# A hybrid GLA and neighbourhood-attention step: gate tiles dealt over five steps, and probabilities divided by their sums ahead of the transposes

## The chip, the cores and the metric

The kernel runs on one core of one Trainium2 chip. The metric is the device time of one execution in microseconds (us), lower is better; the median of the runs is compared.

## What is computed

One layer of a diffusion backbone over 512 latent tokens (an 8 x 64 grid) and 128 context tokens, width 1024, all in fp32. The reference, cut to what the change touches:

```python
gq, gk, gv, gr, zf, zb, nq, nk, nv, m_gla, m_na = split_in(h @ w_in)
b_gla = (rmsnorm(o_gla, g_gla) * silu(gr)) @ w_gla_o            # 4 heads of 128
qn, kn = rmsnorm(nq, g_qn), rmsnorm(nk, g_kn)                   # 8 heads of 64
# neighbourhood attention: 8 x 16 window of the grid plus all 256 past context keys
s = concat([q k_rows * scale + bias, q k_ctx * scale])
p = softmax(s)
o = p_loc v_rows + p_ctx v_ctx
mix = (sigmoid(m_gla) * b_gla + sigmoid(m_na) * (o @ w_na_o)) @ w_out
```

Context tokens attend to the 128 context tokens alone.

## The kernel before, in words

The kernel is one program of five queues, written out by hand: PE (matmul), ACT, DVE, POOL and SP (its DMA queue), which wait for each other by semaphores. The activations lie transposed (channels in partitions, 640 tokens in the free dimension). A product in fp32 accuracy is made of three fast ones: each operand is split into a high and a low part (fp32r), and `project` (L638 to L653) issues hi x hi, hi x lo and lo x hi for each of 8 row blocks k of a weight tile: six matmuls of 320 columns for each k. A weight tile comes by SP's DMA into `wraw`, ACT's `hi` writes `whi`, and POOL's `lo` (L503) writes `wlo`.

The change lies in the attention stage. It has 20 steps s, four groups j of five: group j handles two heads (r = 0, 1), and i = s % 5 says which queries. For i = 0 to 3 they are 128 latent tokens (a group of 16 grid columns) that see 2, 3, 3 and 2 near blocks of 128 keys and 2 past blocks; for i = 4 they are the context tokens and see one block. In step s:

- PE issues `scores(s)` into the PSUM tensor PA (near blocks of head r in bank r, the past blocks of both heads in bank 2; L924, L928), then `probabilities(s-1)`, the transposes of the exponentials `sc` by a product with the identity (L946), then `gate_part(s)`, then `values(s-1)`, the products with v (L965).
- DVE takes the scores from PSUM, adds the bias, and finds the row maxima (L1991, L1993, L1999), head by head. Between the heads `sums(s-1)` forms the reciprocal of the previous step's sums and widens it to 64 columns for each head (L1964, L1967).
- PE transposes this widened tile too (L956), ACT copies it to `rin_t` (L1435), and DVE's `normalised` multiplies the values by it into `ona` (L1957).
- ACT copies the transposed exponentials to `pT` (L1406, L1408) and forms the exponentials with their sums (L1415).

`gate_part` is independent work for PE: the eight tiles of the projection for the gate m_gla, two in each group, each cut in two halves of 4 k, at i = 1 to 4. At i = 0 stands `gla_stats` instead, the statistics of one GLA head (L893, into PSUM tensor PJ, which the gate tiles also use); ACT's `gla_rms` (L1367, L1369), DVE's `gla_gate` at i = 1 (L1925, L1928), ACT's `gla_hi` at i = 2 and DVE's `gla_low` at i = 3 (L1920) process it. When a group's heads are complete, ACT's copy to `ona_hi` and DVE's `pair_low` (L1942) split them. POOL adds the masks to the bias table of the next group (three additions, L560) once the maxima of its i = 3 step are there, and then does the `lo` of the next two gate tiles. Before step 0 PE forms four statistics of q and k (L882), ACT their logarithms and exponentials (L1377, L1383), and DVE applies them in `qk_norm(n)` (L1933), n = 0 before the loop and n = 1 to 3 at steps 1 to 3, ahead of the maxima. After step 19 SP may load `ada_rest` (L440, waits for `pv_cp` 20), and the merge follows, whose first projection surrounds `values(19)`.

## Time and profile before

| | us |
|---|---|
| median of three runs | 1044.33 (1043.95 to 1046.63) |
| the profiled execution's own time | 1046.15 |
| its span | 1044.3 |
| PE busy | 1009.4 (97% of the span) |
| DVE, ACT, POOL busy | 566.8, 434.8, 478.7 |
| share of PE in the chain that ended last | 66% |

How to read it: the profile is one execution; times in a timeline are microseconds from the start of its span. A matmul's row lasts until its modelled end, and matmuls overlap, so a piece of PE's work is measured from the start of its first row to the start of the next piece's. Where an engine stood idle, the row says for how long and what released it.

### The profile page before, as it was taken

What the parts mean: (1) busy time and instruction counts of PE and PEld (TensorE: products, weight loads), DVE (VectorE), ACT (ScalarE), POOL (GpSimd) and SP (SyncE); (2) the same over time, 40 slices, a digit from 0 to 9 for tenths busy, and PEclk for the clock granted to TensorE, in tenths of its full rate; (3) what the DMA queues carried; (4) which work ended last, traced back from release to release, by engine and by line L of the source; (5) the groups of instructions that cost most, each with busy time, mean ns of one, the idle gap of its engine ahead of it and who ended that gap; (6) DMA issues with size and microseconds to landing.
All of it is one profiled execution on the core that took longest, in us unless ns stands there. A gap on an engine that the chain in (4) does not pass through costs nothing.

```text
span 1044.3 us, 18987 instructions
## 1 busy us (share of the span) xinstructions
PE 1009.4 (97%) x7435; PEld 935.3 (90%) x7435; DVE 566.8 (54%) x1069; ACT 434.8 (42%) x676; POOL 478.7 (46%) x305
## 2 busy tenths in 40 slices
PE   4999999999999999999999999899999999999998
PEld 3999999998788988999987899899999999788886
DVE  6408269842665653332324799777777778532102
ACT  4244254423756563222232355555555555521110
POOL 1476522223133211333342277788877786333331
PEclk9999999999999999999999999999999999999999
DMA  9964222121011006565525122232222231122231
GB/s 340 300 102 81 81 62 61 42 71 52 11 42 41 22 22 201 182 213 192 189 82 181 41 81 73 77 92 84 82 82 81 82 102 42 61 81 80 79 117 68
DMA packets 130837, 103.70 MB, mean 99 GB/s; under 512 B 5830, under 2 KB 111179, under 8 KB 130763
## 3 DMA queue, kind: packets, MB, share of 16 engines
q1 hardware_dynamic: 125736, 95.14, 29.5%
q0 software_dynamic: 1568, 3.15, 2.0%
q10 hardware_dynamic: 3459, 4.40, 1.2%
q8 instruction: 50, 0.82, 0.3%
q14 instruction: 24, 0.20, 0.1%
HBM read 98.21 MB, written 3.41 MB: 97 GB/s over the span
## 4 chain that ended last, share of the span: by engine, by line
PE 66%; POOL 17%; DVE 6%; issue 3%; DMA 3%; ACT 3%; SPq 2%; DVEq 0%; POOLq 0%; ACTq 0%
PE PJ L646 10%; PE PJ L647 10%; PE PJ L651 10%; POOL behind L606 7%; POOL ahead L606 4%; PE PA L1044 3%; PE PA L1045 3%; PE PA L1043 3%; PE PJ L1043 2%; PE PJ L1044 2%; PE PJ L1045 2%; POOL ahead_val L614 2%; PE PA L965 2%; PE PJ L946 2%; POOL behind_val L614 2%
## 5 line engine op out<-in xcount | busy, mean ns | idle before, releaser
L503 POOL TENSOR_TENSOR wlo<-wraw,whi 128x1024 fp32r<-128x1024 f32 x72 | 181.3, 2518 | 363.2 <-ACT whi L1221 268.4
L646 PE MATMUL PJ<-h_hi,whi 128*128 128x320 f32 x640 | 196.4, 315 | 0.0
L647 PE MATMUL PJ<-h_lo,whi 128*128 128x320 f32 x640 | 193.0, 309 | 0.0
L651 PE MATMUL PJ<-h_hi,wlo 128*128 128x320 f32 x640 | 145.9, 309 | 0.0
L646 PEld LDWEIGHTS PJ<-h_hi,whi 128*128 128x128 f32 x640 | 120.4, 188 | 2.6 <-issue 1.6
L647 PEld LDWEIGHTS PJ<-h_lo,whi 128*128 128x128 f32 x640 | 120.6, 188 | 0.0
L1221 ACT ACTIVATE whi<-wraw 128x1024 fp32r<-128x1024 f32 x51 | 53.9, 1059 | 147.7 <-PE PJ L651 78.4
L651 PEld LDWEIGHTS PJ<-h_hi,wlo 128*128 128x128 f32 x640 | 107.2, 188 | 0.0
L1597 ACT ACTIVATE whi<-wraw 128x1024 fp32r<-128x1024 f32 x21 | 22.2, 1059 | 105.6 <-PE PJ L1045 54.0
L2162 DVE SCALAR_TENSOR_TENSOR PJ<-u_all,vec,PJ 128x641 f32<-128x641 f32 x44 | 39.1, 888 | 41.8 <-ACT PJ L1549 41.8
L1164 PE MATMUL PA<-h_hi,behind 128*128 128x320 f32 x192 | 59.3, 309 | 0.0
L606 POOL TENSOR_TENSOR behind<-behind_val,behind 128x512 fp32r<-128x512 f32 x40 | 51.4, 1307 | 1.1 <-ACT behind L1576 1.1
L560 POOL TENSOR_TENSOR bias<-bias,window 128x512 f32<-128x512 f32 (+1 forms) x12 | 19.6, 1658 | 64.8 <-DVE mx_loc L1993 64.8
L1045 PE MATMUL PA<-whi,prod_lo 128*128 128x512 f32 x124 | 48.3, 389 | 0.0
L1162 PE MATMUL PA<-h_hi,ahead 128*128 128x320 f32 x128 | 40.7, 318 | 1.6 <-DVE u_all L2236 0.6
L1576 ACT ACTIVATE behind<-behind_val 128x512 fp32r<-128x512 f32 x40 | 25.0, 625 | 40.1 <-POOL behind_val L614 37.7
L1549 ACT ACTIVATE PJ<-u_all,vec 128x641 f32<-128x641 f32 x44 | 38.9, 884 | 4.6 <-DVE u_all L2228 2.5
L1162 PE MATMUL PA<-h_hi,behind 128*128 128x320 f32 x128 | 39.6, 310 | 0.5 <-issue 0.5
L2165 DVE SCALAR_TENSOR_TENSOR PJ<-u_all,vec,PJ 128x641 f32<-128x641 f32 x44 | 39.2, 890 | 1.5
L1163 PE MATMUL PA<-h_lo,ahead 128*128 128x320 f32 x128 | 39.6, 309 | 0.0
L1163 PE MATMUL PA<-h_lo,behind 128*128 128x320 f32 x128 | 39.6, 309 | 0.0
L1162 PE MATMUL PA<-T_hi,ahead 128*128 128x320 f32 x128 | 39.6, 309 | 0.0
(438 smaller groups left out, 2816.0 us busy)
## 6 DMA issues: line engine op xcount, KB each, us to landing
wraw<-in_w_in_dram SPq DMA_DIRECT2D x82, 256.0 KB, 3.1
ada_rest<-in_w_ada_dram SPq DMA_DIRECT2D x32, 512.0 KB, 5.8
wraw<-in_w_up_dram SPq DMA_DIRECT2D x48, 256.0 KB, 3.6
wraw<-in_w_down_dram SPq DMA_DIRECT2D x42, 256.0 KB, 2.9
raw_even<-in_w_up_dram SPq DMA_DIRECT2D x40, 256.0 KB, 3.6
ada<-in_w_ada_dram SPq DMA_DIRECT2D x8, 1024.0 KB, 9.6
wraw<-in_w_out_dram SPq DMA_DIRECT2D x16, 256.0 KB, 2.8
out_dram<-x ACTq DMA_DIRECT2D x10, 256.0 KB, 2.1
```

The costliest lines, as they stand in the source:

```text
L503: pool.tensor_tensor(wlo[:, slot, 0:k, :], wraw[:, slot, 0:k, :], whi[:, slot, 0:k, :].bitcast(F32), ALU.subtract).then_inc(lo_done, 1)
L606: pool.tensor_tensor(unit_lo[name], value_of(j, name), unit_hi[name].bitcast(F32), ALU.subtract).then_inc(lo_done, 1)
L646: pe.matmul(out, whi[:, slot, w0 + k, :], hi(k)[:, tok], start=start and k == k0, stop=False)
L647: pe.matmul(out, whi[:, slot, w0 + k, :], lo(k)[:, tok], start=False, stop=False)
L651: mm = pe.matmul(out, wlo[:, slot, w0 + k, :], hi(k)[:, tok], start=False, stop=stop and k == k1 - 1)
L1043: pe.matmul(psum(*bank), act_hi_[:, k, tok], w_hi, start=start, stop=False)
L1044: pe.matmul(psum(*bank), act_hi_[:, k, tok], w_lo, start=False, stop=False)
L1045: return pe.matmul(psum(*bank), act_lo_[:, k, tok], w_hi, start=False, stop=stop)
L1162: pe.matmul(out, w_hi[:, k, :], b_hi[:, k, :], start=k == 0, stop=False)
L1163: pe.matmul(out, w_hi[:, k, :], b_lo[:, k, :], start=False, stop=False)
L1164: mm = pe.matmul(out, w_lo[:, k, :], b_hi[:, k, :], start=False, stop=k == 3)
L1221: act.activation(whi[:, slot, :, :], wraw[:, slot, :, :], ACT.Copy).then_inc(hi_done, 1)
```

## The change

- The gate tiles are dealt over all five steps of a group (`GATE_K`): 2, 3 and 3 k for the first tile and 4 and 4 for the second.
- `weights(s)` on DVE multiplies the exponentials themselves (128 x 128 to 128 x 640 for each head) by the reciprocals of their sums, first thing in step s + 1, and PE's transposes wait for it. The widened tile, its transpose and `rin_t` are gone, and `values_out` on ACT copies the finished values.
- Where a step has two near blocks, the past blocks lie in the same bank as the near ones of their head, and the wait on `past_ps` is gone.
- `gla_stats` goes to PA; at i = 0 it follows the gate part, and the scores of i = 1 wait for its logarithm. The fourth q/k statistic moves behind the scores of step 0. On ACT its logarithm and `gla_rms(0)` come before the loop, two exponentials go into steps 1 and 2, and the copy to `ona_hi` comes one step earlier. On DVE `qk_norm(1..3)` and `pair_low` move behind the maxima.

```diff

-GATE_K = {1: (0, 0, 4), 2: (0, 4, 8), 3: (1, 0, 4), 4: (1, 4, 8)}
+GATE_K = [(0, 0, 2), (0, 2, 5), (0, 5, 8), (1, 0, 4), (1, 4, 8)]
 N_LEVEL = 8
...
         rin = at("rin", R + 143072, [2, 2])
-        rin_wide = at("rin_wide", R + 3584, [2, HD])
-        rin_t = at("rin_t", R + 4096, [P])

...
+        def past_at(i, r):
+
+            return 2 * BANK + r * PAST if KEYS[i][1] == 3 else r * BANK + 2 * P
         def halves(ps, pair):
...
-            for n in range(4):
+            def qk_stats(n):
+
                 pe.wait_ge(sqq_set, n + 1)
...
                 elif n >= 2:
-                    pe.wait_ge(sq_ln, n - 1)
+                    pe.wait_ge(sq_ln, 2 * n - 3)
                 for x in range(2):
...
                         o = (2 * x + b) * BANK
-                        mm = pe.matmul((PJ if n % 2 == 0 else PA)[:, o:o + HALF], blk64[:, :],
+                        mm = pe.matmul((PA if n == 1 else PJ)[:, o:o + HALF], blk64[:, :],
                                        qk_rs[n][:, x, b * HALF:(b + 1) * HALF], start=True, stop=True)
...
+            for n in range(3):
+                qk_stats(n)
+
             def gla_stats(hd):
...
                 pe.wait_ge(og_sqd, hd + 1)
-                pe.wait_ge(gate_cp, 2 * hd)
-                if hd == 0:
-                    pe.wait_ge(sq_ln, 4)
+                pe.wait_ge(sc_mx, 10 * hd + 2)
                 for b in range(2):
-                    mm = pe.matmul(PJ[:, b * BANK:b * BANK + HALF], ones[:, :], og_rs[:, b * HALF:(b + 1) * HALF],
+                    mm = pe.matmul(PA[:, b * BANK:b * BANK + HALF], ones[:, :], og_rs[:, b * HALF:(b + 1) * HALF],
                                    start=True, stop=True)
...
                 if s == 0:
-                    pe.wait_ge(sq_ln, 4)
+                    pe.wait_ge(sq_ln, 2)
                 else:
                     pe.wait_ge(sc_mx, 2 * s)
+                if i == 1:
+                    pe.wait_ge(og_ln, j + 1)
                 near = [(0, b) for b in range(nt)]
...
                     for r, (kind, b) in ((0, first), (1, second)):
-                        if r == 0 and kind == 1 and b == 0:
-                            pe.wait_ge(past_ps, j * 4 + i + 1)
+                        if r == 0 and kind == 1 and b == 0 and nt == 3:
+                            pe.wait_ge(past_ps, j * 2 + i)
                         hs = slice(64 * r, 64 * r + 64)
...
                         else:
-                            o = 2 * BANK + r * PAST + b * P
+                            o = past_at(i, r) + b * P
                             mm = pe.matmul(PA[:, o:o + P], q, kcT[hs, j, b * P:(b + 1) * P], start=True, stop=True)
-                            if r == 1 and b == 1:
+                            if r == 1 and b == 1 and nt == 3:
                                 mm.then_inc(past_ps, 1)
...
                 nb = KEYS[i][1] + 2 if i < 4 else 1
-                pe.wait_ge(sc_exp, 2 * s + 2)
+                pe.wait_ge(weight_set, s + 1)
                 if s:
...
                 pe.wait_ge(pt_cp, s + 1)
-                pe.wait_ge(wide_set, s + 1)
                 if s:
                     pe.wait_ge(pv_cp, s)
-                pe.transpose(PA[:, 3 * BANK + P:3 * BANK + 2 * P], rin_wide[:, :, :].rearrange("p r n -> p (r n)"), ident[:, :])
                 col = [(2 * j + r) * HD for r in range(2)]
...
                 j, i = s // 5, s % 5
-                if i == 0:
-                    gla_stats(j)
-                    return
                 b, k0, k1 = GATE_K[i]
                 n = 2 * j + b
+                if s == 0:
+                    qk_stats(3)
+                    gla_stats(0)
+                    pe.wait_ge(sq_ln, 4)
                 if k0 == 0:
-                    pe.wait_ge(og_ln, j + 1)
                     pe.wait_ge(gate_cp, n)
...
                         start=k0 == 0, stop=k1 == 8, done=tile_ready if k1 == 8 else None)
+                if i == 0 and s:
+                    gla_stats(j)
...
             qk_ln(2)
-            qk_ln(3)
             qk_exp(1)
             gla_square(0)
-            qk_exp(2)
-            qk_exp(3)
+            qk_ln(3)
+            gla_rms(0)
             act.wait_ge(nvt_cp, NT)
...
+            def values_out(s):
+
+                i = s % 5
+                act.wait_ge(pv_ps, s + 1)
+                if s == 0:
+                    act.wait_ge(stored, 32)
+                elif i == 0:
+                    act.wait_ge(on_lo, s // 5)
+                o = PA[:, 3 * BANK:3 * BANK + P]
+                if i < 4:
+                    act.activation(ona[:, 0:SAMPLE].rearrange("p (r g c) -> p g r c", g=4, c=GC)[:, i],
+                                   o.rearrange("p (r c) -> p r c", c=GC), ACT.Copy).then_inc(pv_cp, 1)
+                else:
+                    act.activation(ona[:, SAMPLE:TOK], o, ACT.Copy).then_inc(pv_cp, 1)
             on_constant()
-            for s in range(22):
+            for s in range(21):
                 i = s % 5
...
                                        accum_out=psm[:, s % 2, r:r + 1]).then_inc(sc_exp, 1)
-                    if i == 0:
+                    if i == 0 and s:
                         gla_rms(s // 5)
+                    if s in (1, 2):
+                        qk_exp(s + 1)
                     if i in (2, 4):
...
                 if 1 <= s <= 20:
-                    act.wait_ge(pv_ps, s)
-                    act.activation(rin_t[:, :], PA[:, 3 * BANK + P:3 * BANK + 2 * P], ACT.Copy).then_inc(rint_set, 1)
+                    values_out(s - 1)
                 if s < 20 and i == 2:
...
                     gla_square(s // 5 + 1)
-                if s >= 6 and i == 1:
-                    act.wait_ge(pv_cp, s - 1)
+                if s >= 5 and i == 0:
+                    act.wait_ge(pv_cp, s)
                     act.activation(ona_hi[:, s // 5 - 1, :], ona[:, :], ACT.Copy).then_inc(on_hi, 1)
...
-            def normalised(s):
-
-                i = s % 5
-                dve.wait_ge(pv_ps, s + 1)
-                dve.wait_ge(rint_set, s + 1)
-                if s == 0:
-                    dve.wait_ge(stored, 32)
-                elif i == 0:
-                    dve.wait_ge(on_lo, s // 5)
-                out = ona[:, 0:SAMPLE].rearrange("p (r g c) -> p g r c", g=4, c=GC)[:, i] if i < 4 else ona[:, SAMPLE:TOK]
-                o, w = PA[:, 3 * BANK:3 * BANK + P], rin_t[:, :]
-                if i < 4:
-                    o, w = (x.rearrange("p (r c) -> p r c", c=GC) for x in (o, w))
-                dve.tensor_tensor(out, o, w, ALU.mult).then_inc(pv_cp, 1)
-
-            def sums(s):
+            def weights(s):

+                n = (KEYS[s % 5][1] + 2) * P if s % 5 < 4 else P
                 dve.wait_ge(sc_exp, 2 * s + 2)
-                if s:
-                    dve.wait_ge(pv_ps, s)
+                if s >= 2:
+                    dve.wait_ge(weight_set, s - 1)
                 dve.reciprocal(rin[:, s % 2, :], psm[:, s % 2, :]).then_inc(rin_set, 1)
...
                 for r in range(2):
-                    ins = dve.tensor_scalar(rin_wide[:, r, :], ones[:, 0:HD], rin[:, s % 2, r:r + 1], None, ALU.mult)
-                ins.then_inc(wide_set, 1)
+                    ins = dve.tensor_scalar(sc[:, s % 2, r, 0:n], sc[:, s % 2, r, 0:n], rin[:, s % 2, r:r + 1], None, ALU.mult)
+                ins.then_inc(weight_set, 1)
...
                 i = s % 5
-                if s >= 7 and i == 2:
-                    pair_low(s // 5 - 1)
-                if s in (1, 2, 3):
-                    qk_norm(s)
-                if s >= 2:
-                    normalised(s - 2)
+                if 1 <= s <= 20:
+                    weights(s - 1)
                 if s < 20:
...
                         m = slice(r, r + 1)
-                        if r == 1 and s:
-                            sums(s - 1)
                         if i < 4:
...
                             b0 = KEYS[i][2]
-                            dve.tensor_scalar(sc[:, s % 2, r, n:n + PAST], PA[:, 2 * BANK + r * PAST:2 * BANK + (r + 1) * PAST],
+                            dve.tensor_scalar(sc[:, s % 2, r, n:n + PAST], PA[:, past_at(i, r):past_at(i, r) + PAST],
                                               HD ** -0.5, None, ALU.mult, ALU.max, accum_out=mx_ctx[:, s % 2, m])
...
                     gla_gate(s // 5)
+                if s >= 6 and i == 1:
+                    pair_low(s // 5 - 1)
                 if s < 20 and i == 3:
                     gla_low(s // 5)
+                if s in (1, 2, 3):
+                    qk_norm(s)
                 if s == 20:
-                    sums(s - 1)
                     dve.wait_ge(sc_mx, 40)
...
                     dve.tensor_copy(cond_rest[:, :, 0:2], cond2[:, :, :]).then_inc(cond_again, 1)
```

DVE, from step 2 to 3 of the first group: before, and now (`qk_rs_116` is the tile of `qk_norm(3)`, L1933 or L1954; `ISA` is the biased maximum). Before:

```order
L1933 SCALAR_TENSOR_TENSOR nqk<-nqk,vec,qk_rs_116 128x640 [waits sq_rs]
L1933 SCALAR_TENSOR_TENSOR nqk<-nqk,vec,qk_rs_116 128x640
L1957 TENSOR_TENSOR ona<-PA,rin_t 128x8x16 [waits rint_set,pv_ps]
L1991 TENSOR_SCALAR sc,mx_ctx<-PA 128x256 [waits pt_ps,sc_ps]
L1993 ISA sc,mx_loc<-PA,bias 128x256
L1993 ISA mx_loc 128x1
L1996 TENSOR_SCALAR nmx<-mx_loc,mx_ctx 128x1 [waits sc_mx]
L1964 RECIPROCAL rin<-psm 128x2 [waits pv_ps,sc_exp]
L1967 TENSOR_SCALAR rin_wide<-ones,rin 128x64 [waits rin_set]
L1967 TENSOR_SCALAR rin_wide<-ones,rin 128x64
L1991 TENSOR_SCALAR sc,mx_ctx<-PA 128x256
L1993 ISA sc,mx_loc<-PA,bias 128x256
```

Now:

```order
L1992 TENSOR_SCALAR sc,mx_ctx<-PA 128x256
L1994 ISA sc,mx_loc<-PA,bias 128x256
L1994 ISA mx_loc 128x1
L1997 TENSOR_SCALAR nmx<-mx_loc,mx_ctx 128x1 [waits sc_mx]
L1941 TENSOR_TENSOR og_lo<-oT,og_hi 128x640 [waits og_hid]
L1954 SCALAR_TENSOR_TENSOR nqk<-nqk,vec,qk_rs_116 128x640 [waits sq_rs]
L1954 SCALAR_TENSOR_TENSOR nqk<-nqk,vec,qk_rs_116 128x640
L1971 RECIPROCAL rin<-psm 128x2 [waits weight_set,sc_exp]
L1974 TENSOR_SCALAR sc<-sc,rin 128x512 [waits rin_set]
L1974 TENSOR_SCALAR sc<-sc,rin 128x512
L2000 TENSOR_SCALAR sc,mx_ctx<-PA 128x128 [waits pt_ps,sc_ps]
L2003 TENSOR_SCALAR nmx<-mx_ctx 128x1 [waits sc_mx]
```

`qk_norm(3)` stood ahead of the maxima of step 3; now it stands between `gla_low` and the weights of step 3, which are 512 columns wide.

PE at step 5, the first of the second group. Before (L893 is the statistics, L956 the widened tile):

```order
L946 MATMUL PJ<-ident,sc 128x128 [waits pt_cp,sc_exp]
L946 MATMUL PJ<-ident,sc 128x128
L893 MATMUL PJ<-og_rs,ones 128x320 [waits gate_cp,og_sqd]
L893 MATMUL PJ<-og_rs,ones 128x320
L956 MATMUL PA<-ident,rin_wide 128x128 [waits pv_cp,wide_set,pt_cp]
L965 MATMUL PA<-pT,nv_tok 64x128 x2
L924 MATMUL PA<-nqk 128x128 [waits sc_mx]
```

Now, from the end of the gate's 2 k (L648, L649, L653), which began behind the transposes:

```order
L653 MATMUL PJ<-h_hi,wlo 128x320 x2
L648 MATMUL PJ<-h_hi,whi 128x320
L649 MATMUL PJ<-h_lo,whi 128x320
L648 MATMUL PJ<-h_hi,whi 128x320
L649 MATMUL PJ<-h_lo,whi 128x320
L653 MATMUL PJ<-h_hi,wlo 128x320 x2
L897 MATMUL PA<-og_rs,ones 128x320 [waits sc_mx,og_sqd]
L897 MATMUL PA<-og_rs,ones 128x320
L969 MATMUL PA<-pT,nv_tok 64x128 [waits pv_cp,pt_cp]
L969 MATMUL PA<-pT,nv_tok 64x128
L930 MATMUL PA<-nqk 128x128 [waits og_ln,sc_mx]
```

The statistics (L897) come after gate work and write PA, and the next scores (L930) wait for `og_ln`.

ACT ahead of and in step 0. Before (L1377 logarithm, L1383 exponential of q/k; L1363 square, L1367 and L1369 of the GLA head; L1415 exponentials of the scores):

```order
L1377 ACTIVATE qk_rs_115<-PJ,eps 128x1280 [waits sq_ps]
L1377 ACTIVATE qk_rs_116<-PA,eps 128x1280 [waits sq_ps]
L1383 ACTIVATE qk_rs_114<-qk_rs_114 128x1280 [waits sq_ln]
L1363 ACTIVATE og_rs<-oT 128x640
L1383 ACTIVATE qk_rs_115<-qk_rs_115 128x1280 [waits sq_ln]
L1383 ACTIVATE qk_rs_116<-qk_rs_116 128x1280 [waits sq_ln]
L1397 DMA out_dram<-nv_tok 128x512 [waits nvt_cp]
L1415 ACTIVATE sc,psm<-sc,nmx 128x512 [waits sc_cp,const_set]
L1415 ACTIVATE sc,psm<-sc,nmx 128x512 [waits sc_cp]
```

Now:

```order
L1383 ACTIVATE qk_rs_115<-PJ,eps 128x1280 [waits sq_ps]
L1389 ACTIVATE qk_rs_114<-qk_rs_114 128x1280 [waits sq_ln]
L1369 ACTIVATE og_rs<-oT 128x640
L1383 ACTIVATE qk_rs_116<-PJ,eps 128x1280 [waits sq_ps]
L1373 ACTIVATE og_rs<-PA,eps 128x640 [waits og_st]
L1375 ACTIVATE og_rs<-og_rs 128x640 [waits og_ln]
L1402 DMA out_dram<-nv_tok 128x512 [waits nvt_cp]
L1435 ACTIVATE sc,psm<-sc,nmx 128x512 [waits sc_cp,const_set]
L1435 ACTIVATE sc,psm<-sc,nmx 128x512 [waits sc_cp]
```

The fourth logarithm (on `qk_rs_116`) and the GLA head's two operations stand between the second q/k exponential and the first exponentials of the scores.

## Rows read from the trace of the kernel before

**Rows 1.** Timeline of PE (start, us of one row, line, out<-in, shapes)

```profile
301.21 0.44 PE L946 MATMUL PJ<-ident,sc 128*128 128x128 f32 x2
...
333.56 0.44 PE L946 MATMUL PJ<-ident,sc 128*128 128x128 f32 x2
333.83 1.24 PE L893 MATMUL PJ<-og_rs,ones 128*128 128x320 f32 x4
335.51 0.30 PE L956 MATMUL PA<-ident,rin_wide 128*128 128x128 f32 x1 [0.43 <-issue]
...
344.69 0.33 PE L946 MATMUL PJ<-ident,sc 128*128 128x128 f32 x1
...
345.81 0.39 PE L646 MATMUL PJ<-h_hi,whi 128*128 128x320 f32 x1
...
349.41 0.27 PE L956 MATMUL PA<-ident,rin_wide 128*128 128x128 f32 x1
349.61 0.33 PE L965 MATMUL PA<-pT,nv_tok 128*64 128x128 f32 x2
...
350.86 0.37 PE L924 MATMUL PA<-nqk 64*128 64x128 f32 x1
...
352.28 0.33 PE L946 MATMUL PJ<-ident,sc 128*128 128x128 f32 x1
...
365.92 0.33 PE L946 MATMUL PJ<-ident,sc 128*128 128x128 f32 x1
...
396.86 0.33 PE L946 MATMUL PJ<-ident,sc 128*128 128x128 f32 x1
```

**Rows 2.** Waits in the attention stage, 267 to 401 us (total, times, longest)

```profile
PEld PA L928 <- PE PA L928: 2.1, 8, 0.3
```

**Rows 3.** Timelines of DVE, POOL and ACT, 353 to 362 us

```profile
353.35 0.15 DVE L1964 RECIPROCAL rin<-psm 128x2 f32<-128x2 f32 x1
...
353.87 0.41 DVE L1991 TENSOR_SCALAR_CACHE_REDUCE sc<-PA 128x256 f32<-128x256 f32 x1
...
354.80 2.45 DVE L1920 TENSOR_TENSOR og_lo<-oT,og_hi 128x640 fp32r<-128x640 f32 x1
...
359.70 2.49 DVE L1967 TENSOR_SCALAR rin_wide<-ones,rin 128x64 f32<-128x64 f32 x2
...
354.72 4.90 POOL L560 TENSOR_TENSOR bias<-bias,window 128x768 f32<-128x768 f32 x3 [19.52 <-DVE mx_loc L1993]
359.58 2.40 POOL L503 TENSOR_TENSOR wlo<-wraw,whi 128x1024 fp32r<-128x1024 f32 x1
...
355.52 0.72 ACT L1415 ACTIVATE sc<-sc,nmx 128x512 f32<-128x512 f32 x1
```

**Rows 4.** Timelines at the start of the stage

```profile
261.82 3.15 DVE L1933 SCALAR_TENSOR_TENSOR nqk<-nqk,vec,qk_rs 128x640 f32<-128x640 f32 x2 [3.56 <-ACT qk_rs L1383]
...
265.55 1.33 ACT L1377 ACTIVATE qk_rs<-PA,eps 128x1280 f32<-128x1280 f32 x1 [0.82 <-PE PA L882]
...
267.02 0.34 PE L924 MATMUL PA<-nqk 64*128 64x128 f32 x1 [1.51 <-ACT qk_rs L1377]
```

**Rows 5.** Groups of instructions by line and form, DVE

```profile
L1727 DVE TENSOR_SCALAR x_rows<-x_rows,x_rs 128x1024 f32<-128x1024 f32 x5 | 3.4, 749 | 1.7 <-ACT x_rs L1255 1.7
```

**Rows 6.** Windows (granted clock: third value from the end) and PE at 667.68

```profile
268.70:271.70 3.00, 2.99 (x8) 1.74 (x10) 2.93 (x12) 3.00 (x5) 0.00 (x0) 0.50 0.01 3
333.50:335.60 2.10, 1.67 (x11) 0.97 (x7) 1.85 (x9) 1.25 (x4) 1.70 (x1) 1.00 0.00 0
667.90:671.00 3.10, 3.10 (x13) 3.10 (x13) 2.18 (x6) 2.27 (x4) 1.78 (x2) 0.50 0.01 3
...
667.68 0.51 PE L1162 MATMUL PJ<-h_hi,ahead 128*128 128x320 f32 x1 [2.20 <-DVE u_all L2236]
```

**Rows 7.** Timelines of SP's queue and PE at the stage's end

```profile
401.82 2.20 SPq L440 DMA_DIRECT2D ada_rest<-in_w_ada_dram  x4
...
411.58 0.65 PE L1001 MATMUL PA<-ada_rest,cond_rest 128*32 128x128 f32 x16 [0.66 <-DMA ada_rest<-in_w_ada_dram]
```

More of the change, by code:

```diff
@@ L356, in hybrid_dit_step @@
             "bias_set", "sqq_set", "sqk_set", "sq_ps", "sq_ln", "sq_rs", "nqk_set", "ko_ps", "ko_cp", "ko_stored"))
-        sc_ps, sc_mx, sc_cp, sc_exp, pt_ps, pt_cp, pv_ps, past_ps, rin_set, wide_set, rint_set, pv_cp, gate_cp = (sem(n) for n in (
-            "sc_ps", "sc_mx", "sc_cp", "sc_exp", "pt_ps", "pt_cp", "pv_ps", "past_ps", "rin_set", "wide_set", "rint_set", "pv_cp", "gate_cp"))
+        sc_ps, sc_mx, sc_cp, sc_exp, pt_ps, pt_cp, pv_ps, past_ps, rin_set, weight_set, pv_cp, gate_cp = (sem(n) for n in (
+            "sc_ps", "sc_mx", "sc_cp", "sc_exp", "pt_ps", "pt_cp", "pv_ps", "past_ps", "rin_set", "weight_set", "pv_cp", "gate_cp"))
         on_hi, on_lo = sem("on_hi"), sem("on_lo")
@@ L1366, in gla_rms @@
                 act.wait_ge(og_st, hd + 1)
-                act.activation(by_half(og_rs[:, :]), halves(PJ, 0), ACT.Ln, bias=eps[:, :], scale=1.0 / DV).then_inc(og_ln, 1)
+                act.activation(by_half(og_rs[:, :]), halves(PA, 0), ACT.Ln, bias=eps[:, :], scale=1.0 / DV).then_inc(og_ln, 1)
                 act.wait_ge(og_ln, hd + 1)
@@ L1377, in qk_ln @@
                 act.activation(qk_rs[n][:, :, :].rearrange("p x (b n) -> p (x b) n", b=2),
-                               (PJ if n % 2 == 0 else PA)[:, :].rearrange("p (b n) -> p b n", b=4)[:, :, 0:HALF], ACT.Ln,
+                               (PA if n == 1 else PJ)[:, :].rearrange("p (b n) -> p b n", b=4)[:, :, 0:HALF], ACT.Ln,
                                bias=eps[:, :], scale=1.0 / HD).then_inc(sq_ln, 1)
@@ L2013, in _ @@
                     dve.tensor_copy(cond_rest[:, :, 0:2], cond2[:, :, :]).then_inc(cond_again, 1)
-            pair_low(3)
             dve.wait_ge(pt_ps, 20)
@@ L2054, in _ @@
             dve.wait_ge(og_st, 4)
-            dve.wait_ge(wide_set, 20)
             dve.tensor_copy(ffn_rows[:, :, :], rows_all[:, 6:8, :]).then_inc(rows_kept, 1)
```

## The prediction

> **What bounds the kernel now.** The page's busy shares name TensorE (PE), as the small profile above shows. The change touches only the attention stage, so I read PE's timeline there, taking each piece from the start of one group of matmuls to the start of the next [rows 1]. A step is PE-bound almost everywhere: from 344.69 the transposes of a 5-block step take 1.12 us, a gate half-tile (4 k) 3.60, the transpose of the widened reciprocals (L956) 0.20, the values 1.25, the scores 1.42, and the next step follows at 352.28 with nothing between. A full group of five steps takes 365.92 - 333.56 = 32.36 us. PE stands idle only at i = 0, where the values wait after the statistics (335.51, 0.43 us in the row), and, as the waits show, 0.26 us in each of eight score steps, where a past product waits for one of the other head in the same bank [rows 2]. So the questions are what leaves PE, and whether the new order on the other engines makes PE wait. For that I read DVE, ACT and POOL through the i = 3 step that begins at 352.28 [rows 3], the start of the stage [rows 4], the granted clock [rows 6] and the end [rows 7].
>
> I call T0 to T4 the moments at which PE starts its transposes in the five steps of a group (352.28 is a T3).
>
> **What leaves PE.** Twenty transposes of 0.20 us: 4.0 us [rows 1]. The wait between banks in the eight steps with two near blocks, 0.26 us each: 2.1 us [rows 2]; such scores then take 1.15 us. The gate's work is the same, 16 k in a group at 3.60 / 4 = 0.90 us each; only its places change.
>
> **What DVE gets.** The widening goes and two multiplications of 128x512 or 128x640 come, and PE's transposes now wait for them. A tensor_scalar with SBUF on both sides took 749 ns for 1,024 columns [rows 5], so a 640-column one is an estimate of 0.55 us and a 512-column one of 0.48; a pair with its reciprocal costs 1.2 or 1.05 us. The multiplication by rin_t moves to ACT as a copy that takes the place of the copy into rin_t: ACT's work is unchanged, DVE loses 0.3 us a step. Four steps of five hide the new latency. At i = 2, the longest, ACT's exponentials end 4.5 us after T2 (at i = 3 they end 4.15 after T3, at 356.43 [rows 3], and these have 256 columns more), the weights at 5.8, and PE has 1.12 + 2.70 + 1.25 + 1.15 = 6.2 us of other work. At i = 1 gla_gate and the low part of the pair stand in front on DVE; the weights are ready 5.9 us after T1 and PE comes at 6.0.
>
> **The step that isn't hidden is i = 3.** There POOL adds the bias of the next group. The rows show what that does to DVE [rows 3]: an L1920 that asked at 354.80, just after POOL's 4.90 us of additions had begun, took 2.45 us, and at 359.70 two 64-column tensor_scalar took 2.49 us (1,024 columns take 0.75 alone [rows 5]) because POOL's wlo subtraction (2.40 us from 359.58) ran. They alternate: each DVE operation of that kind waits for one of POOL's, and POOL's next for it (the same at the start, where two L1933 take 3.15 us [rows 4]). The Trainium skill (SBUF — State Buffer, section "Who interferes with whom") says that a tensor_scalar between SBUF operands holds a port pair that GpSimd shares, that whichever starts first keeps it for its whole instruction, and that one with only PSUM as source doesn't contend. By that rule the 512-column weights are blocked as the 64-column ones are, and the sum below stands; were they taken to be free, because no row of before has them, it would be 7.5 us lower (rival B). In a middle group: POOL began 2.44 us after T3 (354.72 less 352.28); without the sums between the two heads' maxima (353.35 to 353.87) it begins at T3 + 1.9. gla_low gets through at T3 + 4.4, the first weight multiplication behind the second addition at 5.8, the second behind the third at T3 + 7.3. PE arrives at T4 = T3 + 1.12 + 3.60 + 1.25 + 0.4 = 6.4: it **waits 0.9 us**.
>
> **A middle group.** i = 0: transposes 0.27, 2 k of gate 1.80, statistics 1.24 [rows 1], then ACT's logarithm, 0.8 (an estimate, from 1.33 for twice the columns [rows 4]), which the next scores now wait for since the statistics stand in PA; the context's values are under it; scores 1.42. With hops 5.6. i = 1: 0.9 + 2.70 + 1.0 + 1.42 = 6.0. i = 2: 6.2. i = 3: 6.4. i = 4: wait 0.9 + 0.9 + 3.60 + 1.0 + 1.15 = 7.55. (A 4-block piece is four fifths of the 5-block one.) Together 31.75 against 32.36: **-0.6 us**, twice. The last group has no additions and no wait: from T0 to the last transposes 5.6 + 6.0 + 6.2 + 6.4 + 5.5 = 29.7 against 396.86 - 365.92 = 30.94: **-1.2 us**.
>
> **The first group** is scheduled anew. Scores(0) need only nqk (DVE's L1933 end at 264.97) and two logarithms; they start at 265.05, not at 267.02 [rows 4], and end at 266.2. The fourth qk statistics follow (2.15 us, an estimate from the 1.24 of half as many, to 268.35), their logarithm on ACT to 269.9, then the gate's first 2 k to 271.8 and scores(1) to 273.2. But ACT does that logarithm and gla_rms (0.8 twice) before the exponentials of step 0 (0.7 each and a read-out): these end at 272.8, weights(0) at 273.95, so PE waits 0.6. From 274.0: 0.9 + 2.7 + 1.0 + 1.42 = 280.0; then PE waits 0.5 for weights(1), since gla_gate and qk_norm(1) stand before them on DVE; 1.1 + 2.7 + 1.25 + 1.15 bring T3 to 286.7; there it waits 0.4 for values_out(1), behind hi() on ACT; 1.1 + 3.6 + 1.25 + 0.4 bring T4 to 293.5. Then the worst place: on DVE gla_low, **both** operations of qk_norm(3) and then weights(3) follow, and each takes its turn with POOL's three additions and wlo: additions from 288.6, gla_low 291.1, qk_norm 292.9 and 294.75, wlo till 297.0, weights(3) at 297.8. PE waits **4.2 us**. Before, qk_norm(3) stood ahead of the maxima, where POOL was free. Step 4's 6.65 brings T0 of the next group to 304.45; it was 301.21: **+3.2 us**.
>
> **The end.** The last values stand 0.20 us and a wait of 0.2 earlier behind the merge's first matmuls, and one copy lies between them and pv_cp, not two operations: from the last transposes to SP's issue of ada_rest I get 4.15 us for 401.82 - 396.86 = 4.96. PE waits for that load at 411.58 [rows 7], so all of it counts: **-0.8 us**.
>
> So far 3.2 - 0.6 - 0.6 - 1.2 - 0.8 = 0.0.
>
> **The clock.** After 1.51 us of idleness [rows 4] PE's granted clock was 0.50 (the 1.2 GHz level) from 268.7 to 271.7, and after an idle 2.20 us at 667.68 it was again 0.50 for 3.1 us; at a wait of 0.43 us it stayed at 1.00 [rows 6]. The wait of 4.2 us is longer than both, so some 3.2 us of gate work behind it run at half speed: +1.6 us. At the start PE still idles 1.7 us before scores(0). Before, the slow stretch fell on statistics that PE would have waited after anyway; now the fourth qk statistics, gla_stats and the gate stand there. Bounds: 0.5 us if only gla_stats is hit, 1.6 if the 2.15 us are; I take 1.0. Nothing bounds it below zero, since the old stretch cost nothing.
>
> **Sum: +2.6 us.** Against the profiled execution (1046.15 us, a span of 1044.3 and 1.85 around it) that is 1048.75; that execution lay 1.8 us above the median of the runs, 1044.33, so for the median I say **1046.9**. A measurement of this kernel can tell about 0.3%, 3.1 us, from no change: 1041.2 to 1047.5.
>
> **The rivals.**
> A, the forecast, 0.50; by its bounds 1045.3 to 1048.5.
> B, the port does not matter: the wide multiplications run beside POOL, or the port is granted to whoever is shorter. Then the waits of 4.2 and twice 0.9 go and the 1.6 us of clock: 2.6 - 7.6, 1039.3. For it: no row shows such an operation of 512 columns. Against it: forty L1967 of the same kind, blocked wherever POOL ran. 0.15.
> C, weights(3) get ahead of the wlo subtraction (qk_norm's last operation and the weights taken as one turn): 2.3 us less, 1044.6. Against it stands the strict alternation [rows 3, 4]. 0.13.
> D, slower: **the small waits bring the clock down too.** The waits of 0.6 and 0.9 us at steps 0 and 4 of the middle groups lie between idleness that did no harm (0.4) and one that did (1.51). If the point is below 0.9, each middle group loses 1.6 us more: 2.6 + 3.2, 1050.1. 0.22.
> That the change doesn't do what it says, because the transposes it removes were idle time of PE, is excluded: PE goes on without a gap on either side of them [rows 1].
>
> **Numbers.** Faster by over 0.3%: B and a little of C, 0.17. Slower: D and the upper quarter of A, 0.33. Within: 0.50. The range leaves out most of B (0.15) and what lies above D (0.05): 1041.0 to 1050.8.
>
> **What would show it.** The group length T0 to T0 of 31.7 in the second and third groups and 29.7 in the last; DVE's multiplications of step 3 of 1.3 us and more while POOL adds; PE idle for about 4 us before the transposes of step 4 in the first group and then at 0.50; scores(0) at 265. If the multiplications show 0.5 us while POOL runs, my main step is wrong; if the waits are there but the time falls, the gain on PE is larger than 6 us.

## The result, and the profile after

The changed kernel takes **1048.14 us** (median of 8 runs, 1046.51 to 1049.24); the kernel before, run beside it, 1044.19 (8 runs). The ratio is 1.0035, 95% interval 1.0025 to 1.0045; run again as the control of the experiments it came out at 1.0030 (1.0019 to 1.0041). So it is slower, by about as much as the 0.3% that can be told from no change. The forecast was 1046.9, with a range of 1045.3 to 1048.5. The profiled execution took 1046.54 us, the second shortest of the eight, with a span of 1044.7.

The page (busy time by engine):

```profile
PE 1004.6 (96%) x7415; PEld 932.4 (89%) x7415; DVE 570.5 (55%) x1049; ACT 433.4 (41%) x676; POOL 480.1 (46%) x305
```

PE is busy 4.8 us less than before (1009.4), and yet the kernel is slower: the time went into waits of PE. PE's timeline, read at the same places as in [rows 1]:

```profile
253.86 0.30 PE L870 MATMUL PA<-ident,nvraw 128*128 128x128 f32 x1 [0.45 <-ACT oT L1361]
...
264.36 0.37 PE L930 MATMUL PA<-nqk 64*128 64x128 f32 x1 [1.65 <-DVE nqk L1954]
...
285.99 0.33 PE L952 MATMUL PJ<-ident,sc 128*128 128x128 f32 x1
...
297.00 1.97 PE L952 MATMUL PJ<-ident,sc 128*128 128x128 f32 x8 [4.42 <-DVE sc L1974]
298.62 0.61 PE L648 MATMUL PJ<-h_hi,whi 128*128 128x320 f32 x1
...
303.59 0.66 PE L969 MATMUL PA<-pT,nv_tok 128*64 128x128 f32 x8
...
305.71 0.44 PE L952 MATMUL PJ<-ident,sc 128*128 128x128 f32 x2
...
309.97 0.34 PE L930 MATMUL PA<-nqk 64*128 64x128 f32 x1 [0.60 <-ACT og_rs L1373]
...
331.06 0.33 PE L952 MATMUL PJ<-ident,sc 128*128 128x128 f32 x1 [0.83 <-DVE sc L1974]
...
337.72 0.44 PE L952 MATMUL PJ<-ident,sc 128*128 128x128 f32 x2
...
369.74 0.44 PE L952 MATMUL PJ<-ident,sc 128*128 128x128 f32 x2
...
399.75 0.44 PE L952 MATMUL PJ<-ident,sc 128*128 128x128 f32 x2
```

The row at 264.36 begins scores(0). The 4.42 us before the row at 297.00 are the wait for weights(3) in the first group; behind it the 4 k of gate work take 303.59 - 298.62 = 4.97 us. The middle groups, T0 to T0, take 337.72 - 305.71 = 32.01 and 369.74 - 337.72 = 32.02 us (32.36 before), the last one, to the last transposes, 399.75 - 369.74 = 30.01 (30.94 before). In each middle group there is a wait of 0.83 us at step 4, and one of 0.60 us for gla_rms's logarithm at step 1.

What DVE and POOL do in the first of these waits (their timelines):

```profile
287.99 2.46 DVE L1941 TENSOR_TENSOR og_lo<-oT,og_hi 128x640 fp32r<-128x640 f32 x1
290.37 3.70 DVE L1954 SCALAR_TENSOR_TENSOR nqk<-nqk,vec,qk_rs 128x640 f32<-128x640 f32 x2
293.99 0.15 DVE L1971 RECIPROCAL rin<-psm 128x2 f32<-128x2 f32 x1
294.18 2.77 DVE L1974 TENSOR_SCALAR sc<-sc,rin 128x512 f32<-128x512 f32 x2
...
287.90 5.49 POOL L562 TENSOR_TENSOR bias<-bias,window 128x768 f32<-128x768 f32 x3 [24.28 <-DVE mx_loc L1994]
293.35 2.92 POOL L505 TENSOR_TENSOR wlo<-wraw,whi 128x1024 fp32r<-128x1024 f32 x1
```

gla_low, qk_norm(3) and the first multiplication of weights(3) are stretched while POOL's additions and subtraction run from 287.90 to 296.27; the second multiplication, behind POOL's end, is short (2.37 and 0.47 us of the pair's 2.77). Over the stage the forms show it (groups by line and form, total and mean ns of one):

```profile
L1974 DVE TENSOR_SCALAR sc<-sc,rin 128x512 f32<-128x512 f32 x16 | 12.6, 829 | 0.3
L1974 DVE TENSOR_SCALAR sc<-sc,rin 128x640 f32<-128x640 f32 x16 | 8.1, 551 | 0.3
```

The shorter form is the slower one on average, since half of its sixteen stand in the steps i = 3 (the others in i = 0), and in three of these four steps POOL is adding.

The granted clock (windows; third value from the end), behind the start of scores(0) and around the long wait:

```profile
264.30:267.00 2.70, 2.64 (x22) 2.13 (x23) 1.40 (x9) 1.55 (x2) 0.00 (x0) 1.00 0.00 0
267.00:270.00 3.00, 2.66 (x13) 1.76 (x12) 0.49 (x3) 2.06 (x3) 0.00 (x0) 1.00 0.00 0
...
292.00:294.00 2.00, 0.58 (x8) 0.30 (x4) 2.00 (x3) 0.28 (x1) 2.00 (x2) 1.00 0.00 0
294.00:296.00 2.00, 0.00 (x0) 0.00 (x0) 1.96 (x3) 0.00 (x0) 2.00 (x1) 0.66 0.01 4
296.00:298.00 2.00, 1.00 (x5) 1.01 (x6) 1.67 (x8) 0.00 (x0) 0.26 (x1) 0.50 0.17 19
298.00:300.00 2.00, 2.00 (x10) 2.00 (x9) 0.00 (x0) 1.00 (x2) 0.00 (x0) 0.50 0.83 243
300.00:302.00 2.00, 2.00 (x11) 2.00 (x10) 0.65 (x3) 0.79 (x5) 0.00 (x0) 0.64 0.00 0
302.00:304.00 2.00, 2.00 (x20) 1.81 (x20) 0.00 (x0) 0.30 (x1) 0.00 (x0) 1.00 0.00 0
```

It falls to 0.50 (the 1.2 GHz level) at about 294.6, some 2.0 us into the idleness, and stays there to about 301.4; nowhere else in the stage is it below 1.00, the start included.

At the end PE's load of ada_rest is there when it comes, and the 64 matmuls stand in one piece, unlike [rows 7]:

```profile
404.03 2.20 SPq L442 DMA_DIRECT2D ada_rest<-in_w_ada_dram  x4
...
411.67 2.01 PE L1007 MATMUL PA<-ada_rest,cond_rest 128*32 128x128 f32 x64
```

### The profile page after: what moved, and what is told of

Read it like the earlier page. It is cut to its first block, busy times and chain, and to the rows that moved or that the text cites. A ratio compares the mean times of both kernels' runs of the same rounds, so it can differ in the third digit from the quotient of the medians.

```text
span 1044.7 us, 18913 instructions
## 1 busy us (share of the span) xinstructions
PE 1004.6 (96%) x7415; PEld 932.4 (89%) x7415; DVE 570.5 (55%) x1049; ACT 433.4 (41%) x676; POOL 480.1 (46%) x305
## 4 chain that ended last, share of the span: by engine, by line
PE 61%; POOL 19%; DVE 8%; issue 4%; ACT 3%; DMA 3%; SPq 2%; DVEq 0%; POOLq 0%; ACTq 0%
PE PJ L648 10%; PE PJ L649 9%; PE PJ L653 9%; POOL behind L608 8%; POOL ahead L608 4%; PE PA L1049 3%; PE PA L1050 3%; PE PA L1051 3%; POOL ahead_val L616 2%; PE PJ L1049 2%; PE PJ L1050 2%; PE PJ L1051 2%; POOL behind_val L616 2%; PE PA L786 2%; PE PA L1007 1%
## 5 line engine op out<-in xcount | busy, mean ns | idle before, releaser
L648 PE MATMUL PJ<-h_hi,whi 128*128 128x320 f32 x640 | 197.4, 316 | 0.3 <-ACT qk_rs L1383 0.3
L649 PE MATMUL PJ<-h_lo,whi 128*128 128x320 f32 x640 | 193.5, 310 | 0.0
L653 PE MATMUL PJ<-h_hi,wlo 128*128 128x320 f32 x640 | 146.2, 310 | 0.0
L648 PEld LDWEIGHTS PJ<-h_hi,whi 128*128 128x128 f32 x640 | 120.9, 189 | 3.4 <-issue 1.6
L649 PEld LDWEIGHTS PJ<-h_lo,whi 128*128 128x128 f32 x640 | 121.1, 189 | 0.0
L653 PEld LDWEIGHTS PJ<-h_hi,wlo 128*128 128x128 f32 x640 | 107.4, 189 | 0.0
```

The costliest lines, as they stand in the source:

```text
L648: pe.matmul(out, whi[:, slot, w0 + k, :], hi(k)[:, tok], start=start and k == k0, stop=False)
L649: pe.matmul(out, whi[:, slot, w0 + k, :], lo(k)[:, tok], start=False, stop=False)
L653: mm = pe.matmul(out, wlo[:, slot, w0 + k, :], hi(k)[:, tok], start=False, stop=stop and k == k1 - 1)
```

## The experiments

Executions of one kernel differ by 1.2 to 5.2 us (the 35 of the kernel before by 6.5), so beside each median stands the length of the stage in its profile: on PE, from the first transpose of the new values (254.52 before, 253.86 after) to the last transposes of probabilities (396.86 and 399.75).

| kernel | stage, us | against before | median against before (its runs) |
|---|---|---|---|
| before | 142.34 | | |
| changed | 145.89 | +3.55 | +3.95 |
| changed, again | 145.36 | +3.02 | +3.37 |
| fill the wait | 143.87 | +1.53 | +1.07 |
| gate ahead (two profiles) | 142.08, 142.10 | -0.26, -0.24 | +1.02, +0.26 |
| norm later | 140.13 | -2.21 | -2.78 |
| bias later (two profiles) | 137.51, 137.52 | -4.83, -4.82 | -4.55, -4.76 |
| bias later, rms early | 136.01 | -6.33 | -5.72 |
| before, bank only | 140.97 | -1.37 | -0.81 |
| before, no wide transposes | 141.05 | -1.29 | -0.40 |

The two columns agree within 1.3 us everywhere: that is how well one profile stands for a median of 5 to 12 executions. The stage as measured here leaves out its end, the load of `ada_rest`.

**The changed kernel again.** 

> The changed kernel itself once more, unaltered, as the control beside which the edits of this group stand, and for a second profile. The first profile lay at 1046.5 us, the median of its runs at 1048.1; stage by stage it lost 2.1 us in the attention stage, where the runs' medians differ by 3.9. Theory 1 (the missing 1.6 us are stretches of low granted clock that come in some executions and not in others): a profile near 1048 shows a stretch at 0.50 that the first did not have, near 268 or near 667 us. Theory 2 (the attention stage itself varies): groups of another length than 32.0, 32.0 and 30.0 us. Median against the kernel before 1.0035 by both.

Measured: median 1048.09 (9 runs), profile 1046.52, the shortest of its runs; the wait is 4.41 us, groups of 32.0, 32.0 and 30.0, no slow stretch near 268 or 667 us. So two profiles of it agree with each other and both lie low, and neither theory is shown. Part of it lies ahead of the stage, where the kernels' instructions are the same: in these two profiles the stage begins at 253.86 and 253.94 us, the earliest of all twelve profiles (their median is 254.5, the latest 255.66). What else the other executions have more was not seen.

The clock falls at another moment than in the first profile (windows):

```profile
296.00:297.40 1.40, 0.34 (x3) 0.34 (x4) 1.36 (x6) 0.00 (x0) 0.33 (x1) 1.00 0.00 0
...
298.00:300.00 2.00, 2.00 (x10) 2.00 (x9) 0.00 (x0) 1.28 (x3) 0.00 (x0) 0.50 0.83 242
```

It holds over the whole wait and falls only when PE, which began again at 297.06, is at work. The low stretch lasts to about 300.9, half as long as in the first profile.

**Norm later.** In the loop over steps on DVE:

```
-                if s in (1, 2, 3):
-                    qk_norm(s)
+                if s in (1, 2, 4):
+                    qk_norm(min(s, 3))
```

> The changed kernel with the fourth pair's qk_norm one step later on DVE: behind the maxima of step 4 instead of between gla_low and the probabilities' multiplications of step 3. Theory 1 (each of its two operations waits for one of POOL's operations, and the multiplications behind them are late for that): PE's wait before the transposes of step 4 in the first group falls from 4.43 us to about 0.8, as in the middle groups, and the granted clock stays at 1.00 behind it; 3.6 + 1.3 = 4.9 us less than the changed kernel, about 1043.2. Rival (POOL's additions and the wlo subtraction set when the multiplications end, whatever stands before them): the wait stays above 3 us and the time at 1048.

Measured: 1041.94 us, ratio 0.9971 (0.9961 to 0.9980): 6.15 us less than the control, where theory 1 gave 4.9. PE's and DVE's timelines at the place:

```profile
293.96 1.09 PE L952 MATMUL PJ<-ident,sc 128*128 128x128 f32 x8 [0.73 <-DVE sc L1974]
...
288.63 2.45 DVE L1941 TENSOR_TENSOR og_lo<-oT,og_hi 128x640 fp32r<-128x640 f32 x1
291.01 0.15 DVE L1971 RECIPROCAL rin<-psm 128x2 f32<-128x2 f32 x1
291.19 2.71 DVE L1974 TENSOR_SCALAR sc<-sc,rin 128x512 f32<-128x512 f32 x2
```

The multiplications are as long as in the changed kernel (2.71 for 2.77) but begin 4.55 us behind T3 (286.64) and not 8.19 (T3 at 285.99), PE waits 0.73, and the clock stays at 1.00. The rival falls. Half a line in another place makes the changed kernel faster than the kernel before.

**Bias later.** On POOL, ahead of the additions for group j:

```
                     pool.wait_ge(sc_mx, 10 * j - 2)
+                    pool.wait_ge(weight_set, 5 * j - 1)
```

> The changed kernel with one wait more on POOL: the additions of the next group's bias begin only when the multiplications of step 3 are done. Theory 1 (DVE's multiplications and POOL's additions take turns on a shared port): the multiplications of step 3 take about 0.48 us each, the waits of 4.43 and twice 0.83 us before the transposes of step 4 go and with the first one the stretch at half clock; 4.4 + 1.3 + 1.7 = 7.4 us less than the changed kernel, about 1040.7. Rival 1 (the multiplications are late for ACT's exponentials or for their own length, not for POOL): the waits stay, 1048. Rival 2 (the additions and the two subtractions behind them now come too late and push against the next multiplications, of step 4, and the first maxima of the next group): the waits at step 4 go and new ones of 1 to 2 us each appear at step 0; 1042 to 1046.

Measured: 1040.17 us, 0.9960 (0.9946 to 0.9974), and in its second run, below, 1039.81. DVE and POOL now (timelines):

```profile
288.50 0.81 DVE L1942 TENSOR_TENSOR og_lo<-oT,og_hi 128x640 fp32r<-128x640 f32 x1
289.23 1.67 DVE L1955 SCALAR_TENSOR_TENSOR nqk<-nqk,vec,qk_rs 128x640 f32<-128x640 f32 x2
290.82 0.15 DVE L1972 RECIPROCAL rin<-psm 128x2 f32<-128x2 f32 x1
291.02 0.88 DVE L1975 TENSOR_SCALAR sc<-sc,rin 128x512 f32<-128x512 f32 x2
...
296.17 2.62 DVE L1975 TENSOR_SCALAR sc<-sc,rin 128x128 f32<-128x128 f32 x2
...
292.04 4.32 POOL L563 TENSOR_TENSOR bias<-bias,window 128x768 f32<-128x768 f32 x3 [27.92 <-DVE sc L1975]
296.32 2.38 POOL L505 TENSOR_TENSOR wlo<-wraw,whi 128x1024 fp32r<-128x1024 f32 x1
```

The same operations take 0.81, 1.67 and 0.88 us where they took 2.46, 3.70 and 2.77, and POOL's three additions 4.32 for 5.49: both engines lose by meeting. All three waits at step 4 are gone (PE goes from the scores at 292.59 to the transposes at 293.01). The meeting moves to weights(4), a pair of 128 columns that takes 2.62 us, but PE needs it only at 299.67. Theory 1 gave 7.4 us; 7.9 were measured. Rival 2 is half seen: weights(4) are pushed back, but PE waits for nothing.

**Gate ahead.** Step 4 of the first group, on PE (gate_part takes the range of k):

```
+                if s == 4:
+                    gate_part(s, (4, 6))
                 if s:
                     probabilities(s - 1)
-                if s < 20:
+                if s == 4:
+                    gate_part(s, (6, 8))
+                elif s < 20:
                     gate_part(s)
```

> The changed kernel with half of one gate half-tile (2 k, 1.84 us) of step 4 of the first group ahead of the transposes of step 3's probabilities instead of behind them; nothing else moves. PE's wait there becomes 4.43 - 1.84 = 2.6 us. Theory 1 (idleness of 2.6 us still brings the granted clock down, as 2.20 us did near 667 us in the kernel before): 1.8 us less than the changed kernel, 1046.3. Theory 2 (it does not, as 1.93 us before the first scores did not): 1.8 + 1.3 = 3.1 us less, 1045.0. Rival (the multiplications are late because of PE's own order): the wait stays at 4.4, 1048.

Measured: 1045.74 us, 1.0009 (0.9998 to 1.0019), 2.35 us less than the control; the wait is 2.48 us.

> The kernel with half of a gate half-tile ahead of the transposes of step 3, a second time, for a second profile. Its first profile showed the wait shortened to 2.48 us and no slow stretch behind it, at 1043.5 us, the lowest of its 12 executions; the others reached to 1046.9. Theory 1 (the clock falls after such a wait in some executions): the profile shows a stretch at 0.50 behind the wait when its time is 1045 or more. Theory 2 (the clock holds after 2.5 us; the spread of 3 us comes from outside the attention stage): no such stretch, and the stage from its first score product to the merge as long as the first time.

Measured: 1045.00 us, 1.0004 (0.9993 to 1.0014), what theory 2 of the first run gave. Its timeline and window:

```profile
298.76 1.09 PE L952 MATMUL PJ<-ident,sc 128*128 128x128 f32 x8 [2.48 <-DVE sc L1980]
...
298.50:303.00 4.50, 4.24 (x43) 3.88 (x45) 1.57 (x10) 3.11 (x7) 0.00 (x0) 1.00 0.46 117
```

In both profiles the clock holds over 2.48 us of idleness, and the stage is equally long (142.08, 142.10). The profiled execution of the second took 1044.4 us, no long one, so that the clock falls in some other execution isn't excluded: in the changed kernel it fell once after 2.0 us of idleness and once only behind 4.41.

**Fill the wait.** Ahead of the wait for weights(3) on PE:

```
+                if s == 3:
+                    pe.wait_ge(pt_cp, s)
+                    for _ in range(32):
+                        pe.transpose(PJ[:, 2 * BANK:2 * BANK + P], ident[:, :], ident[:, :])
                 pe.wait_ge(weight_set, s + 1)
```

> The changed kernel with 32 transposes of the identity (about 3.5 us of PE work whose result is overwritten) put into the first group's wait of 4.43 us before the transposes of step 3's probabilities. The wait for DVE's multiplications is as long as before, but PE idles about 0.9 us of it and not 4.4. Theory 1 (idleness brings the clock down, and the stretch at half clock costs 1.1 to 1.3 us as in the two profiles of the changed kernel): the granted clock stays at 1.00 there and the time is 1.2 us less, 1046.9. Theory 2 (in most executions that stretch costs more than in the two profiled ones, both at the low end of their runs): 2.5 us less, 1045.6. Rival (the clock falls for another reason, or costs nothing): 1048.1.

Measured: 1045.81 us, 1.0013 (1.0004 to 1.0022): 2.3 us less than the control.

```profile
292.61 3.71 PE L946 MATMUL PJ<-ident 128*128 128x128 f32 x32
297.15 1.09 PE L956 MATMUL PJ<-ident,sc 128*128 128x128 f32 x8 [0.82 <-DVE sc L1978]
...
297.00:302.00 5.00, 4.85 (x38) 4.66 (x40) 1.47 (x10) 1.99 (x6) 0.00 (x0) 1.00 0.39 105
```

The multiplications come no earlier; with 32 useless transposes in the wait the clock stays at 1.00 in the profile, and the time is shorter. Transposes and gate are 0.85 and 3.69 us where they were 1.62 and 4.97 (1.28 and 4.83 in the second profile): the fall of the clock cost 1.6 to 2.05 us in the profiles, and by the medians nearer the 2.5 of theory 2.

**Bank only.** The kernel before with `past_at` and the wait for `past_ps` as in the change, and nothing else.

> The kernel before with one part of the change alone: in the eight steps with two near blocks the past products of a head go to the bank of that head's near products, and PE waits for no product of the other head there. Forecast: the scores of such a step take 1.15 us or less, not 1.43, 8 x 0.26 = 2.1 us (8 x 0.34 = 2.7 if they take 1.09 as in the changed kernel): 1042 from 1044.4, ratio 0.9975 to 0.998. Rival (the products were not on the path that sets the end, so PE waits as much longer for the exponentials): no change, 1044.4.

Measured: 1043.93 us, 0.9988 (0.9976 to 0.9999), where 0.9975 to 0.998 was forecast. The scores take 1.09 us in all eight steps, 0.34 less, but the stage gains 1.37, not 2.7. In the scores of i = 0 it only brings PE sooner to a wait (timelines of PE, DVE and POOL):

```profile
333.08 0.44 PE L950 MATMUL PJ<-ident,sc 128*128 128x128 f32 x2
...
335.36 0.30 PE L960 MATMUL PA<-ident,rin_wide 128*128 128x128 f32 x1 [0.56 <-issue]
...
334.33 0.93 DVE L1971 TENSOR_SCALAR rin_wide<-ones,rin 128x64 f32<-128x64 f32 x2
...
332.69 2.36 POOL L507 TENSOR_TENSOR wlo<-wraw,whi 128x1024 fp32r<-128x1024 f32 x1 [3.21 <-ACT whi L1225]
```

The transpose of the widened sums stands behind the widening, and that ends at 335.26, just behind POOL's subtraction (335.05), however early it was asked for: T0 to this row is 2.28 us, and was 335.51 - 333.56 = 1.95 [rows 1], so that all but 0.01 of the 0.34 is given back. The turns with POOL cost the kernel before a little too. The group is 32.02 us.

**No wide transposes.** In the kernel before, `if s == 0:` ahead of the transpose of rin_wide; the kernel then leaves out the sums of all steps but the first, and its output is not the layer's.

> The kernel before without nineteen of the twenty transposes of the widened reciprocals (only step 0 keeps its own; the probabilities' sums of the other steps are therefore not carried to the division, and the attention's values are scaled by those of step 0). Everything else, the widening on DVE, ACT's copy and the multiplication on DVE, stays. Theory 1 (each costs PE its 0.20 us, as the prediction took it): 19 x 0.20 = 3.8 us less, 1040.6. Theory 2 (half of the 0.20 us only stands in for the emptying of PE's pipeline, which the values then show instead; the changed kernel's gate pieces grew from 3.60 to 3.69): 19 x 0.11 = 2.1 us less, 1042.3.

Measured: 1044.34 us, 0.9995 (0.9982 to 1.0008), a stage 1.29 us shorter, a group 32.04 us; the medians alone show no change. The gate's 4 k and the values behind them:

```profile
353.48 0.39 PE L646 MATMUL PJ<-h_hi,whi 128*128 128x320 f32 x1
...
357.17 0.55 PE L966 MATMUL PA<-pT,nv_tok 128*64 128x128 f32 x6
```

3.69 us, where gate and transpose took 3.60 + 0.20 [rows 1]: 0.11 us each, not 0.20, and at i = 0, where PE waits for the widening, the step even takes 0.10 us more (4.12 us from T0 to T1, 4.02 before). Theory 2 is the nearer, and even it promised too much.

**Bias later again, and with gla_stats early.** On top of the bias-later kernel:

```
-                if i == 0 and s:
-                    gla_stats(j)
+                if i == 4 and s < 19:
+                    gla_stats(j + 1)
```

with gla_square at i = 3, the logarithm behind the gate tile's copy on ACT, its exponential behind hi(), and the wait for og_ln at the first scores of the next group.

> The kernel whose additions of the bias begin after the multiplications of step 3, once more, as the control beside the next one and because its nine executions lay between 1038.9 and 1043.0 us. If the mechanism is right: no wait before the transposes of step 4 in any group, groups of 31.1 us, 0.3 to 0.5 per cent faster than the kernel before. If its first result was a lucky profile and median: above 0.998.

> The same with one wait more taken away: gla_stats of the next group moves from step 0 to the end of step 4's gate piece (ACT squares one step earlier, its logarithm follows the gate tile's copy, its exponential the high half), so that the scores of step 1 no longer wait for ACT's logarithm. PE waits 0.61 us there in three groups. Theory 1 (the wait goes and nothing takes its place): 3 x 0.61 = 1.8 us less than the control, near 1038.5. Rival 1 (the wlo subtraction, now later by the logarithm's 0.8 us, takes the port when the multiplications of step 0 want it): the wait comes back before the transposes of step 0's probabilities, 0.3 to 0.9 us a group, 0 to 0.9 us less than the control. Rival 2 (the first scores of a group now wait for the logarithm, since they use its banks): same size, the wait stands before scores of step 0.

Measured: 1039.81 us (0.9953, 0.9939 to 0.9966) and 1038.85 us (0.9946, 0.9933 to 0.9960). The stage is 1.5 us shorter than the control's; the waits of PE in it, from its second profile:

```profile
PE PA L931 <- DVE nqk L1959: 1.7, 1, 1.7
PE PJ L953 <- DVE sc L1979: 0.8, 2, 0.5
PE PA L1035 <- DVE rest_rows L2041: 0.8, 1, 0.8
PE PJ L649 <- ACT qk_rs L1386: 0.3, 1, 0.3
```

The wait for og_rs, 3 x 0.6 us, is no longer listed, and 0.1 us a group of another kind stands in its place. The 1.0 us between these two medians is not more than the spread of five runs can hide; against the kernel before both are faster beyond doubt. This is the best kernel of the study.

## Why the prediction was right, and where not

The time, 1048.1, lies 1.2 us above the forecast and inside its range. What bounds the result was foreseen: the changed order on DVE sends weights(3) behind operations that take turns with POOL. By its steps, from the profile:

- **The first group.** Forecast: scores(0) without the 2 us of waiting, small waits of 0.6, 0.5 and 0.4, and 4.2 us at step 4. In the profile 0.53, 0.32, none, and 4.42. That the 4.2 hang on qk_norm(3) and on POOL is shown by the two experiments that move one and the other.
- **The clock behind it.** 1.6 forecast, for gate work alone; 1.6 to 2.05 seen, 1.1 to 1.3 of it in the gate work and 0.4 to 0.8 in the transposes, which ran at the low level too.
- **The clock at the start.** +1.0 forecast, 0 seen. This is the step that failed: the idleness before scores(0) brought nothing down, in any profile with the new order. Its bounds were 0.5 and 1.6 us, and nothing at all was not among them. Without it the sum is +1.6 and the time 1045.9.
- **T0 of the second group**, counted from the stage's start, came 51.85 us after it (51.35 in the second profile) where it was 301.21 - 254.52 = 46.69: +5.2 (+4.7). Forecast: 3.2 + 1.6 + 1.0 = 5.8.
- **Middle groups** -0.35 each, not -0.6; **the last** -0.93, not -1.2. The term that was mis-sized is that of the transposes: a row of 0.20 us was worth 0.11, nineteen of them made the stage 1.3 us shorter (no-wide run), and in the changed kernel four k of gate work take 3.69 us, not 3.60. For the five transposes of a group some 0.45 us too much was promised (an estimate, 5 x 0.09). The bank change gave 0.34 for each of a group's two scores where 0.26 was taken, 0.16 us the other way. Together that is about the 0.26 us between 31.75 and 32.01. (In the kernel before, the gain at i = 0 is given to a wait behind it, as the bank-only run shows.) The waits were right: 0.83 for 0.9 at step 4, and T0 to T1 with gla_rms's logarithm 311.39 - 305.71 = 5.68 for 5.6.
- **The end.** SP issues the load 4.28 us after the last transposes (4.15 forecast, 4.96 before). In the profile the end, from the last transposes to the merge's next products (413.21 before, 414.67 after), is 16.35 - 14.92 = 1.4 us shorter, more than the 0.8 forecast, but that includes luck of the load: from its first ada_rest matmul to the first row of L1034 (414.42 in the changed kernel) PE took 2.69 to 3.90 us in the twelve profiles, and with the old order alone 2.69, 3.44 and 3.90. On average the end takes 15.1 us in the nine profiles with the new order and 15.7 in the three with the old one, which is near the forecast.
- **Rival B** (the port does not matter) falls: 829 ns for the 512-column form, 484 once POOL is moved (the same group of the bias-later kernel, 7.1 us for 16). The rule the prediction took from the Trainium skill (SBUF — State Buffer, section "Who interferes with whom") holds here for the wide form as it did for the narrow one. What the runs show is that an operation of one engine ends only behind that of the other; what the engines share was not tested. **Rival C** falls: the first multiplication waited for the subtraction. **Rival D** falls: the clock is 1.00 behind the waits of 0.60 and 0.83 us.

From the stage's start to the merge's next products the profile gives 160.81 - 158.69 = +2.1 us where the sum was +2.6, but its terms were off by 1.0 (the clock at the start) and 0.6 (the end) one way, and by 0.25 twice, 0.3 and 0.4 (the rest of the first group) the other: a sum that comes out is no proof of its terms, and that the median lies so near the forecast is in part luck, for the medians differ by 3.95 and 3.37 us and not by 2.6. Three small slips of the prediction change nothing: the exponentials of [rows 3] end at 355.52 + 0.72 = 356.24 and not at 356.43, 297.8 - 293.5 is 4.3 and not 4.2, and rival B's price stands once as 7.5 and once as 7.6 us. What stays open: the other executions of the changed kernel are some 1.6 us longer than the profiled ones. Some 0.6 us of it may be the early start of the stage in both profiles (an estimate from the twelve starts), and part a longer stretch at the low clock, for filling the wait saved 2.3 us by the medians and 1.5 to 2.0 by the profiles.

## What to carry to other kernels

Before an operation on DVE is put on the path to PE, look at what POOL runs at that moment and at what stands ahead of it on DVE: with SBUF on both sides of both, four operations of DVE in turns with four of POOL made PE wait 4.4 us and brought its clock down a level, and moving two of them by a step, or POOL by a semaphore, gave back 6 to 8 us. What a removed instruction is worth is its share of a stretch without gaps, taken as the difference of the stretch with and without it, and not its own row; and a saving in front of a wait is given to the wait, unless the wait's end moves too. When PE must wait long, put work of its own ahead of the wait; even useless matmuls there saved time in this case.
